# Two transformer blocks in float32 on one core: both attention stages rearranged, embedding stages reordered, and the sum of squares of retention taken earlier

## The chip, the cores and the metric

The kernel runs on one core of one Trainium2 chip. The metric is the device time of one execution in microseconds; the times given are the median of three executions and their range. The profile is of one further execution.

## The reference

Two blocks, each of two layers, work on 512 tokens of width 1024, all in float32. What matters here:

```python
# first block, layer 0: retention, 4 heads, q/k 256 wide, v 512 wide
o = o * rsqrt(mean(o * o) + eps) * gn_g          # per head, over its 512 columns
y = (silu(gate) * o) @ w_out
# first block, layer 1: latent attention, 16 heads, keys and values from one latent of width 256
q_cat = concat([q_nope @ w_uk, rope(q_rope)]) * scale
k_cat = concat([c_kv, rope(k_rope)])             # the rope part (64 wide) is shared by all heads
p = softmax(causal(q_cat @ k_cat.T)); o = (p @ c_kv) @ w_uv
# after each layer i of the first block: the embedding stage
x = x + rms_norm(y, post_norm_g[i])
x = x + (p[i] @ ple_w_proj[i]) * sigmoid(x @ ple_w_gate[i])
# second block: chunk gating mixer, MLP, then dilated attention, MLP
# dilated attention: 8 heads of 64, three groups (window, dilation) = (128,1), (512,4), (2048,16)
num = p @ v                                      # unnormalised, summed over the three groups
o = (sum of num * scale) / (sum of den * scale); y = o @ w_out
```

## The kernel before, in words

**Splitting.** Every matmul operand is split into a high part of type fp32r and a low rest, also fp32r. A product is three matmuls, high by high, high by low, low by high (`mm3`, lines 401 to 404). `tile_of` (lines 406 to 420) makes one output tile of 128 x 512 by all products with the high weights first and those with the low weights last; `tiles_together` (lines 422 to 434) makes several tiles in step, so that each part `k` of the moving operand is used by all of them before the next part is waited for.

**Panels.** All weights come as 175 panels of 128 x 2048, in the order in which they are used. SyncE loads panel `m` once the low part of `m - 2` is made; ScalarE makes the high part (`split_panel`, `split_quarter`, lines 1011 to 1026, which wait until TensorE is through with panel `m - 2`), GpSimd the low part in four quarters (line 354). Two slots for each of RAW, WH and WL.

**Engines.** There is no scheduler: each engine has its own list, written out by hand, and they meet in counting semaphores. TensorE writes 8 PSUM banks; before it takes a bank it waits until the last user has freed it (`bank`, line 379, `free`). ScalarE evicts or makes high parts (`hi`, line 1009), VectorE makes low parts (`lo`, line 1571), scales, adds and finds maxima.

**Retention** (`head`, lines 485, 1110, 1658), four times: q, k, v tiles, decayed products, gates, results. The four result tiles are squared by ScalarE, the squares added into SS by VectorE (`ret_squares`). TensorE then has gate tile 2, the matmul of ONES with SS (line 542), gate tile 3, and the two output panels, the first with `tiles_together` on YH and YL (in memory AH and AL). VectorE's order behind the sum is gate 2, reciprocal, the results times the root, low part of y(0), gate 3, and so on (lines 1717 to 1740); ScalarE's is root, tanh of gate 2, high parts of y(0) and y(1).

**Embedding** (`per_layer_input`, lines 561, 1181, 1782), after each layer of the first block: TensorE makes 8 projected tiles from panel `n` (with the sum of squares behind the second), then the gate tiles from panels `n + 1` to `n + 4`. The two tiles of `n + 1` are made together, each part k as soon as VectorE has GL(k) (24 x 512-wide matmuls per tile, 48 for both); the panels behind it come after that. ScalarE splits panel `n + 1` after the root of the norm, and the quarters of panel `n + 2` between its high parts of x.

**Latent attention** (lines 609 to 716, 1267 to 1361, 1840 to 1981), eight pairs of heads, seven of them in a loop. For a head, `mla_scores` (line 638) makes for each of four query tiles, 128, 256, 384 and 512 keys wide, three products of the latent part and three of the rope part. QRH and QRL hold the rope parts of both heads of the pair, 64 partitions each; KRH and KRL hold the key's, once for each head with the other head's partitions zeroed by OF_HEAD. At the end of a pair: `swapped` (line 619, a float32 matmul that exchanges the halves for the rotation), `latent_values`, `mla_weighted` into bank 3, and the output panel with four tiles together and four alone. VectorE's order there: low probabilities, low y(0), `turned` (line 1840: it frees the bank of the straight copy at its second multiplication), low rope, `gated`, low y(1), low values. In front of the first pair VectorE clears all of ACC (line 1882) between `turned` and low rope.

**Dilated attention** (lines 826 to 1000, 1452 to 1552, 2106 to 2289), four pairs of heads. The 36 projected tiles (`unit`) take turns in banks 0 and 1 with the transposed values (units 9 to 11 of `_unit_banks`), the exchanged sums (12) and the rows of inverses (13), each in the bank that comes next. A pair's exponentials and weighted values are made behind the units of the next pair; those of the last pair stand at the end, between the first output tiles. `att_weighted` (line 902) multiplies the values of both heads, 128 columns, with the probabilities of one, 36 matmuls per head: 9 of 256 columns moving and 27 of 128; only the 64 result partitions of the head are used.

Of the kernel before, what the change touches and what calls it, by code (L numbers as in the profile page):

```python
# [8 lines left out]
KD = D_MODEL // 128  # L9
# [79 lines left out]
def _unit_banks():  # L89


    order = []
    for n in range(ATT_PAIRS):
        if n > 0:
            order += [(n, 0), (n - 1, 11), (n, 1)]
        order += [(n, j) for j in range(2, 6)]
        if n > 0:
            order.append((n - 1, 12))
        order += [(n, 6), (n, 7)]
        if n > 0:  # L100
# [5 lines left out]
    banks[ATT_PAIRS - 1, 12], banks[ATT_PAIRS - 1, 13] = 3, 5  # L106
# [34 lines left out]
def program(nc, panels, gains, xin, pin, pos, gn, decay, consts, moves, rel, onehot, wsT, bs, out, scratch, xsave):  # L141
# [5 lines left out]
    with ctx:  # L147
# [40 lines left out]
        with ExitStack() as c:  # L188
            CQH, CQL = sb("CQH", [128, KQ, 512], f32r, c), sb("CQL", [128, KQ, 512], f32r, c)
            CKH, CKL = sb("CKH", [128, KC, 512], f32r, c), sb("CKL", [128, KC, 512], f32r, c)  # L190
            KRH, KRL = sb("KRH", [128, 2, 512], f32r, c), sb("KRL", [128, 2, 512], f32r, c)
            MQH, MQL = sb("MQH", [128, 4, 512], f32r, c), sb("MQL", [128, 4, 512], f32r, c)
            QRH, QRL = sb("QRH", [128, 512], f32r, c), sb("QRL", [128, 512], f32r, c)
# [4 lines left out]
        MU = (SS[:, :], R[:, :])  # L198
        X = sb("X", [128, KD, 512])
# [176 lines left out]
        def _(pe):  # L376
# [29 lines left out]
            def tile_of(o, w, f, width, xh, xl, k0, k1, first=True, last=True, at=0, wait=None):  # L406
# [5 lines left out]
                for k in range(k0, k1):  # L412
# [3 lines left out]
                    nc.tensor.matmul(o, wh[:, columns[k - k0]], xl[:, k, :], start=False, stop=False)  # L416
                for k in range(k0, k1):
# [50 lines left out]
            def bias_rows():  # L468
                pe.wait_ge(S["rel_loaded"], 32)
                pe.wait_ge(S["rel_neg"], 1)  # L470
# [14 lines left out]
            def head(h, first=False):  # L485
# [75 lines left out]
            def per_layer_input(L, n):  # L561
# [13 lines left out]
                for j in range(4):  # L575
                    w = panel(n + 1 + j, (n + 1 + j) % 2)
                    if j == 0:
                        ends = tiles_together([bank(0), bank(1)], w, 256, GH, GL, KD,
                                              lambda k: pe.wait_ge(S["ple_h_split"], KD * L + k + 1))
                        for f, end in enumerate(ends):  # L580
                            signal(end, "ple_gate_made", f == 1)
                        continue
# [424 lines left out]
        def _(act):  # L1007
# [10 lines left out]
            def split_quarter(m, part):  # L1018
# [6 lines left out]
                if part == 3:  # L1025
                    end.then_inc(hi_ready, 1)
# [1448 lines left out]
```

## Time and profile before

| | us |
|---|---|
| median of three executions (range) | 2277.23 (2276.5 to 2277.91) |
| the profiled execution | 2274.16 |
| its span | 2272.1 |
| TensorE matmul busy | 2177.4 (96%) |
| VectorE busy | 1187.4 (52%) |
| GpSimd busy | 969.0 (43%) |
| ScalarE busy | 861.1 (38%) |
| mean granted clock of TensorE | 0.989 |

The profiled execution took 2.1 us more than its span and 3.1 us less than the median. A busy matmul row includes the time that its result takes to arrive, so matmuls overlap: how fast they follow is read from their starts. In rows of the timeline the columns are start, duration, engine, line, operation, output and inputs, form, count, and in brackets the idle time before it with what ended it. PE is TensorE's matmuls, PEld its weight loads, DVE VectorE, ACT ScalarE, POOL GpSimd.

### The profile page before, as it was taken

The numbers are of one execution on the slowest core, as the hardware profiler recorded it, in microseconds if no ns is written. First come the engines' busy times: TensorE is split into PE (matmuls) and PEld (weight loads), VectorE is DVE, ScalarE is ACT, GpSimd is POOL, SyncE is SP. The second block draws the span as 40 slices with busy tenths as digits, with TensorE's granted clock in tenths as the row PEclk, the third lists the DMA queues.
The fourth block names the chain that finished last, engine by engine and source line by source line (L and its number), as shares of the span: only waits on it lengthen the run. The fifth ranks groups of instructions, "written<-read, shape, count | busy, mean of one in ns | idle before, by whom it ended". The sixth has DMA issues, their size and how long they took to land.

```text
span 2272.1 us, 29536 instructions
## 1 busy us (share of the span) xinstructions
PE 2177.4 (96%) x10336; PEld 1803.3 (79%) x10336; DVE 1187.4 (52%) x1714; ACT 861.1 (38%) x1264; POOL 969.0 (43%) x706
## 2 busy tenths in 40 slices
PE   7999999898999999988999999999999989999997
PEld 6888878687888888866888888887788777888885
DVE  7655556866666666667265222225465456222224
ACT  4423323544444444444444223224334444223323
POOL 4453444455433333324445544554433223544453
PEclk9999999999999999999999999999999999999998
DMA  5222222132222222212322232224221211222221
GB/s 173 86 98 79 92 78 92 66 132 92 77 82 81 74 74 74 86 72 92 113 73 95 93 105 98 92 92 130 75 75 56 75 56 56 93 92 98 105 92 56
DMA packets 37838, 200.03 MB, mean 88 GB/s; under 512 B 4331, under 2 KB 9707, under 8 KB 15372
## 3 DMA queue, kind: packets, MB, share of 16 engines
q1 hardware_dynamic: 28496, 188.76, 23.7%
q10 hardware_dynamic: 9276, 10.37, 1.5%
q8 instruction: 44, 0.72, 0.1%
q14 instruction: 22, 0.18, 0.0%
HBM read 193.87 MB, written 5.24 MB: 88 GB/s over the span
## 4 chain that ended last, share of the span: by engine, by line
PE 86%; DVE 8%; ACT 2%; DVEq 2%; issue 1%; DMA 0%; SPq 0%; ACTq 0%
PE bank L415 16%; PE bank L416 16%; PE bank L419 16%; PE bank L402 12%; PE bank L403 11%; PE bank L404 11%; ACT WH L1009 1%; PE bank L858 1%; DVE PKL L1571 1%; DVE X L1792 1%; DVE T L1790 1%; PE bank L449 1%; DVE SS L1590 1%; DVE R L1579 1%; DVE T L1719 1%
## 5 line engine op out<-in xcount | busy, mean ns | idle before, releaser
L354 POOL TENSOR_TENSOR WL<-RAW,WH 128x512 fp32r<-128x512 f32 x700 | 965.3, 1410 | 1274.4 <-ACT WH L1009 1274.4
L1009 ACT ACTIVATE WH<-RAW 128x2048 fp32r<-128x2048 f32 (+1 forms) x181 | 335.9, 1856 | 640.7 <-PE bank L419 310.2
L415 PE MATMUL bank<-HH,WH 128*128 128x512 f32 x968 | 387.6, 400 | 8.7 <-DVEq L2231 5.5
L416 PE MATMUL bank<-HL,WH 128*128 128x512 f32 x968 | 379.8, 392 | 0.0
L419 PE MATMUL bank<-HH,WL 128*128 128x512 f32 x968 | 239.1, 389 | 0.0
L415 PEld LDWEIGHTS bank<-HH,WH 128*128 128x128 f32 x968 | 183.4, 189 | 51.2 <-DVEq L2231 5.9
L416 PEld LDWEIGHTS bank<-HL,WH 128*128 128x128 f32 x968 | 183.4, 189 | 39.3 <-issue 2.2
L419 PEld LDWEIGHTS bank<-HH,WL 128*128 128x128 f32 x968 | 181.7, 188 | 37.8
L2078 DVE TENSOR_TENSOR X<-X,bank 128x512 f32<-128x512 f32 x128 | 87.7, 688 | 196.6 <-PE bank L419 117.4
L2069 DVE SCALAR_TENSOR_TENSOR TG<-bank,RS 128x512 f32<-128x512 f32 x64 | 44.0, 688 | 205.1 <-PE bank L404 135.8
L402 PE MATMUL bank<-HH,WH 128*128 128x512 f32 x288 | 112.7, 391 | 5.9 <-DVE HL L1585 5.9
L404 PE MATMUL bank<-HH,WL 128*128 128x512 f32 x288 | 112.1, 389 | 0.0
L403 PE MATMUL bank<-HL,WH 128*128 128x512 f32 x288 | 112.1, 389 | 0.0
L402 PE MATMUL bank<-HIDH,WH 128*128 128x512 f32 x256 | 99.6, 389 | 0.0
L403 PE MATMUL bank<-HIDL,WH 128*128 128x512 f32 x256 | 99.6, 389 | 0.0
L404 PE MATMUL bank<-HIDH,WL 128*128 128x512 f32 x256 | 99.6, 389 | 0.0
L415 PE MATMUL bank<-HIDH,WH 128*128 128x512 f32 x256 | 99.6, 389 | 0.0
L416 PE MATMUL bank<-HIDL,WH 128*128 128x512 f32 x256 | 99.6, 389 | 0.0
L1571 DVE TENSOR_TENSOR HIDL<-T,HIDH 128x512 fp32r<-128x512 f32 x64 | 54.7, 857 | 68.8 <-ACT HIDH L1009 65.6
L402 PE MATMUL bank<-WH,HH 128*128 128x512 f32 x192 | 74.9, 390 | 0.9 <-ACT O L1009 0.9
L404 PE MATMUL bank<-WH,HL 128*128 128x512 f32 x192 | 74.7, 389 | 0.0
L403 PE MATMUL bank<-WL,HH 128*128 128x512 f32 x192 | 74.7, 389 | 0.0
(416 smaller groups left out, 4444.6 us busy)
## 6 DMA issues: line engine op xcount, KB each, us to landing
RAW<-panels SPq DMA_DIRECT2D x175, 1024.0 KB, 4.8
X<-xin SPq DMA_DIRECT2D x4, 512.0 KB, 9.6
xsave<-X ACTq DMA_DIRECT2D x4, 512.0 KB, 2.8
X<-xsave ACTq DMA_DIRECT2D x1, 2048.0 KB, 8.5
TAB<-scratch ACTq DMA_DIRECT2D x16, 128.0 KB, 3.0
out<-ACC SPq DMA_DIRECT2D x8, 256.0 KB, 2.5
RS<-decay ACTq DMA_DIRECT2D x4, 256.0 KB, 2.5
scratch<-O SPq DMA_DIRECT2D x4, 256.0 KB
```

The source lines that it names most:

```text
L354: gp.tensor_tensor(WL[:, s, cs], RAW[:, s, cs], WH[:, s, cs].bitcast(f32), ALU.subtract).then_inc(lo_ready, 1)
L402: nc.tensor.matmul(o, ah, bh, start=start, stop=False)
L403: nc.tensor.matmul(o, ah, bl, start=False, stop=False)
L404: return nc.tensor.matmul(o, al, bh, start=False, stop=stop)
L415: nc.tensor.matmul(o, wh[:, columns[k - k0]], xh[:, k, :], start=first and k == k0, stop=False)
L416: nc.tensor.matmul(o, wh[:, columns[k - k0]], xl[:, k, :], start=False, stop=False)
L419: end = nc.tensor.matmul(o, wl[:, columns[k - k0]], xh[:, k, :], start=False, stop=last and k == k1 - 1)
L449: end = nc.tensor.matmul(o[:, :], wl[:, columns[k][i]], xh[:, k, :], start=False, stop=k == nk - 1)
L1009: return nc.scalar.activation(dst, src, ACT.Copy)
L1571: return v.tensor_tensor(dst, src, high.bitcast(f32), ALU.subtract)
L2069: v.scalar_tensor_tensor(TG[:, f % 2, :], B[f][:, :], 0.0, RS[:, :], ALU.max, ALU.mult)\
L2078: end = v.tensor_tensor(X[:, f, :], X[:, f, :], B[b][:, :], ALU.add)
```

## The change

Six things are done at once.

- Retention: the matmul of the sum of squares is issued inside gate tile 2, between its products with high and with low weights. VectorE takes gate 2 after y(0)'s low part instead of ahead of the reciprocal; ScalarE takes the tanh of gate 2 after the high parts of y(0) and y(1).
- Embedding: between the parts k of the first two gate tiles TensorE issues high products of a third tile, from the panel behind, and all of the fourth tile's high products ahead of the low ones. ScalarE loads the table of the root ahead of the squares, splits panel `n + 1` in quarters around the last square, and the quarters of `n + 2` one high part earlier each, the last one after all high parts of x.
- Latent attention, scores: QR holds for head `a` the high query part in its own 64 partitions and the low part in the other 64; KRH is not masked any more (both halves hold the same key). One matmul of QR with KRH is then high by high and low by high, and QR with the masked KRL is high by low: two matmuls for three. High and low rope parts take two instructions of 64 partitions each.
- Latent attention, order: ScalarE's straight copy frees its bank itself; five output tiles together instead of four; low rope after low y(1) on VectorE; on ScalarE high y(1) ahead of high rope and the next panel's split last; ACC cleared in two pieces, ahead of the root of the latent norm and between two low parts.
- Dilated attention, banks: values of groups 1 and 2 in banks 6 and 7, inverse rows in bank 4, so that banks 0 and 1 are left to the units, the values of group 0 and the exchanged sums. At the end, the transposes of the last pair's probabilities come right behind its last unit, and its values of group 2 after the weighted values of group 0.
- Dilated attention, weighted values: only the head's 64 value columns are loaded as weights, with the result always in partitions 0 to 63.

Two semaphores of the bias rows at the very start are merged into one.

```diff
@@ _unit_banks
-        if n > 0:
-            order += [(n, 0), (n - 1, 11), (n, 1)]
-        order += [(n, j) for j in range(2, 6)]
+        order += [(n, j) for j in range(6)]
         if n > 0:
             order.append((n - 1, 12))
-        order += [(n, 6), (n, 7)]
-        if n > 0:
-            order.append((n - 1, 13))
-        order += [(n, 9), (n, 8), (n, 10)]
-    order.append((ATT_PAIRS - 1, 11))
+        order += [(n, 6), (n, 7), (n, 9), (n, 8)]
...
+    for n in range(ATT_PAIRS):
+        banks[n, 10], banks[n, 11], banks[n, 13] = 6, 7, 4
@@ TensorE, retention
-                end = tile_of(bank(2)[:, :], w, 0, 256, HH, HL, 0, KD)
+                end = tile_of(bank(2)[:, :], w, 0, 256, HH, HL, 0, KD, between=sum_of_results)
                 end.then_inc(S["ret_g_made"], 1)
-                o = bank(4)
-                pe.wait_ge(S["ret_squares"], h + 1)
-                nc.tensor.matmul(o[:, :], ONES[:, :], SS[:, :], start=True, stop=True).then_inc(S["ret_sum"], 1)
@@ TensorE, embedding
+                for k in range(KD):
+                    pe.wait_ge(S["ple_h_split"], KD * L + k + 1)
+                    for f in range(2):
...
+                        end = mm3(os_[f][:, :], w0[0][:, c:c + 128], w0[1][:, c:c + 128], GH[:, k, :], GL[:, k, :],
+                                  k == 0, k == KD - 1)
...
+                    if k >= 2:
+                        if k % 2 == 0:
+                            pe.wait_ge(S["ple_gate_quarter"], 3 * L + k // 2)
+                        high_products(0, k - 2)
+                pe.wait_ge(hi_ready, n + 3)
+                high_products(0, KD - 2)
+                high_products(0, KD - 1)
+                os_.append(bank(3))
+                for k in range(KD):
+                    high_products(1, k)
@@ TensorE, latent attention
-                    mm3(o, QRH[:, qs], QRL[:, qs], KRH[:, a, 0:m], KRL[:, a, 0:m], False, True)\
-                        .then_inc(S["mla_s_made"], 1)
+                    nc.tensor.matmul(o, QR[:, a, qs], KRH[:, 0:m], start=False, stop=False)
+                    nc.tensor.matmul(o, QR[:, a, qs], KRL[:, a, 0:m], start=False, stop=True).then_inc(S["mla_s_made"], 1)
-                ends = tiles_together([bank(4 + f) for f in range(4)], w, 1024, MYH, MYL, 2,
+                ends = tiles_together([bank(b) for b in (4, 5, 6, 7, 1)], w, 1024, MYH, MYL, 2,
@@ TensorE, dilated attention
-                        vs = slice(128 * r, 128 * r + 128)
+                        vs = slice(128 * r + 64 * e, 128 * r + 64 * e + 64)
-                            end = mm3(o[:, rs], vh, vl, DPH[:, e, rs], DPL[:, e, rs], g == 1 and r == 0, g == 2 and r == 3)
+                            end = mm3(o[0:64, rs], vh, vl, DPH[:, e, rs], DPL[:, e, rs], g == 1 and r == 0, g == 2 and r == 3)
@@ TensorE, its end
                 unit(n, 8)
+                if n == ATT_PAIRS - 1:
+                    att_transposes(n, 0)
                 value_transposes(n, 1)
-            value_transposes(last, 2)
             os_ = [bank(0)]
             out_tile(os_[0], 0, 0, last)
-            att_transposes(last, 0)
             os_.append(bank(1))
             out_tile(os_[1], 1, 0, last)
             att_weighted(last, 0)
+            value_transposes(last, 2)
@@ ScalarE, embedding
+                nc.scalar.activation(EPSC[:, 3:4], EPSC[:, 0:1], ACT.Sqrt)
+                squares(f"post{L}", KD, y_made, lambda: split_quarter(n + 1, 0))
+                for part in range(1, 4):
+                    split_quarter(n + 1, part)
+                root(f"post{L}", D_MODEL)
...
+                for k in range(3, KD):
+                    if k % 2 == 1:
+                        split_quarter(n + 2, (k - 3) // 2, "ple_gate_quarter")
+                    high_x(k)
+                split_quarter(n + 2, 3)
@@ ScalarE, latent attention
+            def straight(b, dst):
+                nc.scalar.activation(dst, B[b][:, :], ACT.Copy).then_inc(S["mla_straight"], 1)
+                act.drain().then_inc(free[b], 1)
...
                 high_y(0)
+                high_y(1)
                 if not last:
                     act.wait_ge(S["mla_rope_f32"], n * 1 + 3)
-                    hi(QRH[:, :], TG[:, 0, :]).then_inc(S["mla_rope_hi"], 1)
-                    split_in(n, 4, N_MLA + 6)
-                high_y(1)
-                if not last:
+                    high_rope()
                     act.wait_ge(S["mla_o_made"], n * 2 + 2)
                     high_values(n + 1, (2, 0), n * 4 + (N_MLA + 5))
+                    split_in(n, 4, N_MLA + 6)
@@ ScalarE, end of dilated attention
-            high_values(last, 2)
+            high_probabilities(last, 0)
             exponentials(last, 1)
-            high_probabilities(last, 0)
             exponentials(last, 2)
             near_results(last)
+            high_values(last, 2)
@@ VectorE, latent attention
+            v.memset(ACC[:, 0:KQ, :], 0.0)
             inverse_root("ckv")
...
+            v.memset(ACC[:, KQ:KQ + KC, :], 0.0)
             low_qk(0, "k1", 2, FIRST)
-            v.memset(ACC[:, :, :], 0.0)
             low_rope(0)
...
             def low_rope(n):
+                for a in range(2):
+                    ve.wait_ge(S["mla_rope_hi"], n * 2 + (a + 2))
+                    end = lo(QR[own[1 - a], a, :], TG[own[a], 0, :], QR[own[a], a, :])
```

## Rows read from the trace of the kernel before

**Rows 1.** The page of the profile: the span, and TensorE's busy time.
```profile
span 2272.1 us, 29536 instructions
...
PE 2177.4 (96%) x10336; PEld 1803.3 (79%) x10336; DVE 1187.4 (52%) x1714; ACT 861.1 (38%) x1264; POOL 969.0 (43%) x706
```

**Rows 2.** Waits of TensorE: line, what ended them, us in all, times, longest.
```profile
PE bank L402 <- DVE GL L1571: 14.7, 12, 3.5
...
PE bank L402 <- DVE AL L1571: 5.9, 4, 1.5
...
PE bank L402 <- DVE TG L1844: 5.7, 8, 2.1
PE bank L415 <- DVEq L2231: 5.5, 3, 2.0
PE bank L402 <- DVEq L2125: 5.1, 1, 5.1
PE bank L402 <- DVE QRL L1571: 3.4, 1, 3.4
PE bank L415 <- DVEq L2112: 3.2, 7, 0.8
...
PE bank L402 <- DVE MYL L1571: 2.7, 7, 0.4
...
PE bank L837 <- DVEq L2112: 2.1, 4, 0.9
```

**Rows 3.** Timeline of retention's third head: its first output matmul.
```profile
299.98 0.49 PE L402 MATMUL bank<-AH,WH 128*128 128x512 f32 x1 [1.46 <-DVE AL L1571]
```

**Rows 4.** Timeline of the first embedding stage, VectorE.
```profile
431.10 1.53 DVE L1790 SCALAR_TENSOR_TENSOR T<-ACC,G,R 128x512 f32<-128x512 f32 x1 [0.17 <-issue]
...
438.43 0.75 DVE L1790 SCALAR_TENSOR_TENSOR T<-ACC,G,R 128x512 f32<-128x512 f32 x1
...
451.90 3.45 DVE L1571 TENSOR_TENSOR GL<-X,GH 128x512 fp32r<-128x512 f32 x2
```

**Rows 5.** Timeline of TensorE there: first gate matmul, two later tiles' first.
```profile
438.59 0.47 PE L402 MATMUL bank<-GH,WH 128*128 128x512 f32 x1 [1.80 <-DVE GL L1571]
...
456.90 0.39 PE L415 MATMUL bank<-GH,WH 128*128 128x512 f32 x1
...
462.34 0.39 PE L415 MATMUL bank<-GH,WH 128*128 128x512 f32 x1
```

**Rows 6.** Timeline of TensorE: one head's 24 score matmuls, first and next behind.
```profile
738.85 0.22 PE L402 MATMUL bank<-MQH 128*128 128x128 f32 x1
...
742.66 0.39 PE L415 MATMUL bank<-HH,WH 128*128 128x512 f32 x1
```

**Rows 7.** Timeline of VectorE at the end of a pair of latent attention.
```profile
720.71 2.38 DVE L1571 TENSOR_TENSOR PKL<-bank,PKH 128x128 fp32r<-128x128 f32 x4 [3.56 <-ACT PKH L1009]
```

**Rows 8.** Timeline of VectorE ahead of the first pair of latent attention.
```profile
564.76 3.47 DVE L1882 MEMSET ACC<- 128x4096 f32 x1 [0.80 <-issue]
```

**Rows 9.** Windows: PE, PEld, DVE, ACT, POOL busy (x), clock, DMA share, GB/s.
```profile
570.00:575.00 5.00, 5.00 (x19) 4.71 (x19) 4.07 (x10) 1.20 (x4) 5.00 (x5) 0.50 0.54 172
```

**Rows 10.** Groups by form: weight loads of 128 columns and of 24.
```profile
L403 PEld LDWEIGHTS bank<-DPL,DVH 128*128 128x128 f32 x96 | 18.4, 191 | 0.3
...
L472 PEld LDWEIGHTS bank<-TG,ST 33*24 33x24 f32 x4 | 0.3, 99 | 0.8 <-issue 0.7
```

**Rows 11.** TensorE, dilated attention: 24 of `att_weighted`, later scores with 64 rows.
```profile
1751.75 0.22 PE L402 MATMUL bank<-DPH,DVH 128*128 128x128 f32 x1
...
1754.38 0.36 PE L874 MATMUL bank<-SMR,CONST 128*128 128x32 f32 x2
...
1761.05 0.33 PE L858 MATMUL bank<-DKH,DQH 64*128 64x128 f32 x2
1761.21 0.28 PE L858 MATMUL bank<-DKL,DQH 64*128 64x128 f32 x2
```

**Rows 12.** Timeline of VectorE at the end of dilated attention.
```profile
1886.89 0.69 DVE L1571 TENSOR_TENSOR DYL<-TG,DYH 128x512 fp32r<-128x512 f32 x1 [0.70 <-ACT DYH L1009]
```

More of the change, by code:

```diff
@@ L198, in program @@
         MU = (SS[:, :], R[:, :])
+        own = [slice(64 * a, 64 * a + 64) for a in range(2)]
         X = sb("X", [128, KD, 512])
@@ L404, in mm3, with tile_of @@
                 return nc.tensor.matmul(o, al, bh, start=False, stop=stop)
-            def tile_of(o, w, f, width, xh, xl, k0, k1, first=True, last=True, at=0, wait=None):
+            def tile_of(o, w, f, width, xh, xl, k0, k1, first=True, last=True, at=0, wait=None, between=None):
                 wh, wl = w[:2]
@@ L416, in tile_of @@
                     nc.tensor.matmul(o, wh[:, columns[k - k0]], xl[:, k, :], start=False, stop=False)
+                if between is not None:
+                    between()
                 for k in range(k0, k1):
@@ L574, in per_layer_input @@
                         end.then_inc(S["sines"], 1)
-                for j in range(4):
-                    w = panel(n + 1 + j, (n + 1 + j) % 2)
[L577 to L582, printed above, removed]
+                w0, w1 = panel(n + 1, (n + 1) % 2), panel(n + 2, (n + 2) % 2)
@@ new lines, in per_layer_input @@
+                pe.wait_ge(hi_ready, n + 3)
[4 more added lines that the diff above has]
+                    high_products(1, k)
+                for f in range(2):
+                    for k in range(KD):
+                        c = 256 * k + 128 * f
+                        low_up_to(w1, c)
+                        end = nc.tensor.matmul(os_[2 + f][:, :], w1[1][:, c:c + 128], GH[:, k, :], start=False, stop=k == KD - 1)
+                    signal(end, "ple_gate_made", f == 1)
@@ L583, in per_layer_input @@
+                for j in range(2, 4):
+                    w = panel(n + 1 + j, (n + 1 + j) % 2)
                     for f in range(2):
@@ L705, in pair @@
                 w = panel(out_, s1)
-                ends = tiles_together([bank(4 + f) for f in range(4)], w, 1024, MYH, MYL, 2,
+                ends = tiles_together([bank(b) for b in (4, 5, 6, 7, 1)], w, 1024, MYH, MYL, 2,
                                       lambda k: pe.wait_ge(S["mla_y_split"], n * 2 + (k + 1)))
                 for f in range(KD):
-                    end = ends[f] if f < 4 else tile_of(bank((1, 3, 0, 2)[f - 4])[:, :], w, f, 1024, MYH, MYL, 0, 2)
+                    end = ends[f] if f < 5 else tile_of(bank((3, 0, 2)[f - 5])[:, :], w, f, 1024, MYH, MYL, 0, 2)
                     signal(end, "mla_out_made", f == KD - 1)
@@ L1026, in split_quarter @@
                     end.then_inc(hi_ready, 1)
+                elif sig is not None:
+                    end.then_inc(S[sig], 1)
             def split_at(m):
@@ L1033, in split_in, with squares @@
                 split_panel(i * per + m0, m0 % 2, i * (per // 2) + m0 // 2)
-            def squares(name, n, ready):
+            def squares(name, n, ready, in_front_of_last):
                 for k in range(n):
+                    if k == n - 1:
+                        in_front_of_last()
                     src = ready(k)
@@ L1282, in _ @@
             act.wait_ge(panel_used, N_MLA)
-            straight(B[0][:, :], T[:, 2, :])
+            straight(0, T[:, 2, :])
             root("ckv", KV_LORA)
@@ L1854, in low_rope @@
             def low_rope(n):
-                ve.wait_ge(S["mla_rope_hi"], n * 1 + 3)
-                lo(QRL[:, :], TG[:, 0, :], QRH[:, :]).then_inc(S["mla_rope_split"], 1)
+                for a in range(2):
+                    ve.wait_ge(S["mla_rope_hi"], n * 2 + (a + 2))
+                    end = lo(QR[own[1 - a], a, :], TG[own[a], 0, :], QR[own[a], a, :])
+                end.then_inc(S["mla_rope_split"], 1)
             def low_values(n, banks):
@@ L2223, in numerators @@
                     far, near = in_order(B[6 + e], 1), natural(NEAR[:, e, :], 1)
-                    v.tensor_tensor(natural(NUM, 1)[own], near[own], far[own], ALU.add).then_inc(free[6 + e], 1)
+                    v.tensor_tensor(natural(NUM, 1)[own], near[0:64], far[0:64], ALU.add).then_inc(free[6 + e], 1)
                 ve.drain()
```

97 lines of the change are left out of this document (51 added, 46 removed).

## The prediction

> **What bounds the kernel.** I read the page first. TensorE's matmuls are busy for 2177 us of a span of 2272 [rows 1], so what counts is how many matmuls there are, how fast they follow each other, and where TensorE waits. It takes its instructions in order. The second view is the list of waits with TensorE as the one that waits [rows 2]: few are long, and those that this change touches are the twelve for GL in the embedding stages, four for AL in retention, those for TG, MYL and QRL in latent attention, and those that VectorE's queue ends at lines 2231, 2125 and 2112 in dilated attention. The third view is the timeline, for starts. Two tiles of 24 matmuls with 512 columns begin 5.44 us apart [rows 5], so one such matmul costs 5.44 / 24 = 0.227 us. I use start to start throughout, since the duration in a row (0.39) overlaps the next. ScalarE, VectorE and GpSimd are busy half the time or less; they matter only where their chain ends a wait.
>
> The sum is made against the profiled execution, 2274.2 us: its span and 2.1 us around it. The median of the runs is 3.1 us above that, and the saving is taken from the median.
>
> **Retention, 6.0 us.** The output panel waits 1.46 us for y(0)'s low part [rows 3], 5.9 us over four heads [rows 2]. The matmul of the sum now comes ahead of the tile's 8 products with low weights, 8 x 0.227 = 1.8 us earlier; behind it VectorE has one operation of about 0.7 us less before y(0), ScalarE a tanh less. 1.8 + 0.7 is more than 1.46, so the wait goes, with a slower first matmul behind it: 1.5 a head. What is late next is y's parts 2 and 3, each one VectorE operation of some 0.7 us behind the last while TensorE has three matmuls a part and tile; and the squares, needed 1.8 us earlier now. Bounds: 1.0 to 1.6 a head, 4 to 6.5.
>
> **Embedding stages, 12.0 us.** The first two gate tiles begin at 438.59 and their 48 matmuls end at 456.90 [rows 5]: 18.3 us, where 48 x 0.227 = 10.9 would do. The 7.4 us are steps at VectorE's pace, one GL after the other, with 1.8 ahead of the first. The change puts 2 high products of a third tile (0.45 us) behind each part from the third on and 8 more behind, work that TensorE would do anyhow: all 16 fill 16 x 0.227 = 3.6 us of gaps. The rest comes from the quarters of panel `n + 1` going earlier, so that GpSimd's splits lie ahead of VectorE's first operations: with GpSimd busy T takes 1.53 us, without 0.75, and two GL take 3.45 [rows 4]. Three or four such operations give 2 to 3 us, and the high products leave the low ones of the first two tiles to start later, when the last GL is there. Against it: the table of the root is loaded ahead of the squares (which I put at about 1, a guess between nothing and the 1.8 that TensorE waits there), and ScalarE gets a quarter between two squares. 5.6 and 6.4 for the two stages. Bounds: 3.6 a stage, only the products, 7; both stages without a gap, 16.
> Beside the row there is a rule. The Trainium skill, "SBUF — State Buffer", on the engine side, says that VectorE with two SBUF inputs and GpSimd lock their shared port pair for a whole instruction and the loser blocks; 1.53 against 0.75 agrees in kind. By it a split moved away is won in full, which is the upper bound.
>
> **Latent attention, 20.3 us.** A head's scores are 24 matmuls in 742.66 - 738.85 = 3.81 us [rows 6]. One in six goes: 3.81 / 6 = 0.635, for two heads 1.27 a pair. The waits in seven pairs: TG, because the straight copy frees its bank only after VectorE's multiplication, which stands behind low probabilities (2.38 us, themselves 3.56 late [rows 7]), and MYL [rows 2]; (5.7 less the longest, 2.1, which stands before the first pair) / 7 = 0.52, and 2.7 / 7 = 0.39. Freed by ScalarE, and with a fifth output tile of 6 matmuls (1.4 us) between the parts of y, both go; so do two slow restarts, 0.1 each. 1.27 + 0.52 + 0.39 + 0.2 = 2.4, times 7 is 16.7. What moves: low rope goes behind low y(1) on VectorE and waits for ScalarE's high rope, behind which nothing of this pair's output stands; it is due at the next pair's scores, some 7 us on by the timeline. The next panel's high part is last on ScalarE, and GpSimd's quarters behind it, due at the next pair's first `tile_of` [rows 6]. Two instructions of 64 partitions for one of 128 cost up to 0.7 more on VectorE and on ScalarE, under the same cover; without it 1.4 a pair. Last pair: the scores of its first head, 0.6; those of the second lie behind VectorE's maxima.
> Before the first pair TensorE waits 3.4 for QRL and 2.1 for TG [rows 2]. ACC's clearing, 3.47 us right ahead of low rope [rows 8], is moved where VectorE waits. TG's wait and QRL's hang on one chain, so they don't add: about 3.5 less 0.7 for the second rope instruction is 3. The clock is granted at 0.50 there [rows 9], behind the waits, and I leave that as it is. Bounds 1.3 and 4.3. 16.7 + 0.6 + 3 = 20.3.
>
> **Dilated attention, bank order: 10.5 us.** L415 waits 5.5 us for VectorE at 2231 and 3.2 at 2112, line 837 2.1 at 2112 [rows 2]: units and transposes whose bank is still being read. With values and inverses in banks 6, 7 and 4 the units' turn is free of them. 10.8 less 0.6 for what recurs, and 0.3 for restarts. Bounds 5 and 12.
>
> **Dilated attention, narrow weights: 7.0 us.** A head has 9 matmuls of 256 moving columns and 27 of 128, 8 heads, 216 of the latter. 24 of them take 2.63 us, 0.110 each [rows 11], about as long as one with 256 moving columns, so it is the weight load that sets their pace. Loads take 191 ns for 128 columns and 99 for 24 [rows 10], 0.88 ns a column: 56 ns less for 64. 0.110 - 0.056 is 0.054, and 216 x 0.056 = 12. The 72 with 256 columns keep 0.12. A quarter lies in the last pair, whose end is costed below. No row shows 64-column weights. Switches of shape do have rows: scores with 64 rows follow each other by 0.16 after a switch, against 0.11 [rows 11]; 24 stretches of weighted values, two switches each, 0.05 each, is 2.4, of which I take 2 off: (12 x 3 / 4) - 2 = 7. Bounds: 0, no quicker, and 11.
> The Trainium skill speaks against this part twice in "TensorEngine Tiling (Array Packing)": by Key Properties a changed tiling mode drains TensorE, and by Restrictions column tiling disables Fast Weight Load. The first is what the 0.05 shows; by the second a 64-column load might be no quicker than the present 128, which no row here shows, and which is the first rival.
>
> **Dilated attention, its end: 7.0 us.** DYL of the last pair ends at 1887.6 [rows 12], and TensorE had stood 5.1 for the bank at 2125 [rows 2]. The transposes of the last probabilities come behind the last unit instead of behind the first output tile, and the values of group 2 behind the weighted values of group 0. The 5.1 go, and narrow weights shorten what the last chain holds by 4 stretches, some 3 to 4 us. Against it exponentials and low probabilities are needed earlier and TensorE waits there: of 9 I take 7. Bounds 3 and 9. The merged semaphore at the start: nothing, it is a wait on DMA in both.
>
> **Sum.** 6.0 + 12.0 + 20.3 + 10.5 + 7.0 + 7.0 = 62.8; profiled 2211.4, median 2277.2 - 62.8 = 2214.4. I take 2215. All parts good: 6.5 + 16 + 22 + 12 + 11 + 9 = 76.5, 2201. Parts of the sum poor together: 4 + 8 + 16 + 5 + 4 + 3 = 40, 2237.
>
> **Rivals.**
> (1) *Narrow weights load no quicker*. For: no row has them, and the durations of loads overlap matmuls, so 0.88 ns a column is soft. Against: the 0.110 a matmul, with only 128 columns to move, is as slow as with 256, so something else than the moving side sets it, and the load is what is left. Then 7.0 and about 2 in the end go: 2215 + 9 = 2224. Chance 0.15.
> (2) *A wait for the next late item takes the removed one's place*: in the embedding stages the high products wait for a quarter that GpSimd hasn't made, so the change doesn't do what it says there; in a pair TensorE stands for ScalarE's high y(1) or the next panel; in the units for the evicted tile. For: in all these VectorE and ScalarE run at TensorE's pace. Against: they are busy 52 and 38% [rows 1]. Half of embedding (6), the waits of the pairs (7 x 0.9 = 6), 5 of banks, 5 of the end: 22 less, 2237. Chance 0.13.
> (3) *Slower than before*: with 64-column weights a load no longer runs beside the matmul ahead. Place: the 288 matmuls of `att_weighted`; price: 0.19 load [rows 10] + about 0.27 matmul - 0.11 = 0.35 each, 101 us, so 2215 + 9 + 101 = 2325. It makes the sum positive from (62.8 - 9) / 288 = 0.19 us a matmul. Against: scores with 64 rows do overlap [rows 11]. Chance 0.03.
>
> **Chances.** Forecast 0.68, (1) 0.15, (2) 0.13, (3) 0.03; 0.01 for a mishap that leaves the time as it was. A measurement of this kernel can tell some 0.2%, 4.6 us. Forecast, (1) and (2) are all faster: 0.96, same 0.01, slower 0.03. Range: 2200, with all parts good, to 2239, which holds (1) and most of (2).
>
> **Signs in the profile after.** AL gone from TensorE's waits. From first gate matmul to the end of the stretch with the 16 high products about 15 to 16 us (10.9 + 3.6 + 1). A head's scores in 3.17 us, 20 matmuls. TG, MYL, lines 2231 and 2112 gone or under 1. QRL under 1. 24 weighted matmuls in 1.4 us; weight loads of 64 columns at 135 ns. DYL of the last pair 9 us nearer to the stage's start. It would be wrong if PE waits under 402 name GpSimd's quarters, if the stretch of 24 still takes 2.6 us, or if a matmul with narrow weights shows its load in the open.

## The result, and the profile after

The changed kernel took 2204.68 us (median of four runs, 2201.23 to 2208.47), the one before 2276.86; the ratio is 0.9683, with a 95% interval of 0.9665 to 0.9702. Five further runs of it had a median of 2206.72. The forecast was 2215, the range 2200 to 2239. The profiled execution took 2208.5, its span is 2206.7; that of before was 2272.1, so the two profiles differ by 65.4 us, the medians by 72.2.

The page of the changed kernel, head and TensorE's busy time [rows 1]:

```profile
span 2206.7 us, 29453 instructions
...
PE 2148.6 (97%) x10272; PEld 1781.6 (81%) x10272; DVE 1183.2 (54%) x1724; ACT 869.0 (39%) x1279; POOL 960.6 (44%) x706
```

TensorE's waits in the changed kernel (line, what ended them, us in all, times, longest), the head of the list and what answers to [rows 2]:

```profile
PE bank L445 <- ACT WH L1046: 10.4, 1, 10.4
PE bank L401 <- DVE HL L1630: 5.9, 5, 1.7
PE bank L401 <- DVE QR L1616: 5.9, 1, 5.9
...
PE bank L932 <- ACT LG L1522: 2.5, 2, 1.6
...
PE bank L401 <- issue: 1.5, 2, 1.4
...
PE bank L401 <- DVE GL L1616: 1.0, 2, 0.6
...
PE bank L414 <- DVEq L2161: 0.8, 1, 0.8
```

GL fell from 14.7 to 1.0. AL, TG, MYL and the two entries of DVEq with 5.5 and 5.1 are gone; of the 5.3 us at line 2112 0.8 is left. One wait grew: QR before the first pair of latent attention, 5.9 where QRL had 3.4; the prediction's signs had it under 1. It is the place where the waits for T and TG were gathered up (1.9, 2.1 and 3.4 before, one of 5.9 now). Two waits are new, both at the end of dilated attention: 2.5 for LG, ScalarE's exponentials, and one of 1.4 at 1811.7, in front of the weighted values of group 1, which take VectorE's low probabilities.

To see where the time went, I matched the runs of TensorE's matmuls of the two timelines by their operands and compared the starts. Each stage begins and ends at such a start:

| stretch | before, us | after, us | difference | forecast |
|---|---|---|---|---|
| to retention's first scores | 61.74 | 63.42 | +1.7 | 0 |
| retention, to the first embedding stage | 361.34 | 354.91 | -6.4 | -6.0 |
| embedding stage 0, to the norm sum of the next stage | 77.34 | 71.39 | -6.0 | -5.6 |
| from there to the first gate tile of latent attention | 75.20 | 72.48 | -2.7 | -3.0 |
| latent attention from there, to the second embedding stage | 433.67 | 414.29 | -19.4 | -17.3 |
| embedding stage 1 | 77.74 | 70.59 | -7.1 | -6.4 |
| mixer and first MLP | 483.19 | 483.33 | +0.1 | 0 |
| dilated attention, to the last sums' transposes | 272.15 | 255.43 | -16.7 | -17.5 |
| its end, to the MLP | 85.40 | 75.57 | -9.8 | -7.0 |

What is left, +0.9, lies in the last 25 us. The rows are all near their terms. Whether the terms are right inside is what the experiments were for, and there several did not hold. One shift belongs to the borders: the stretch to the first gate tile of latent attention ends behind the scores of the first head, whose saving (0.7 of the 2.7) the forecast books under the pairs.

The +1.7 at the start is not the change's. A window at 40 to 45 us has the granted clock at 0.66, and the same kernel, profiled again, has it at 1.00 (columns as in [rows 9]; first fence the first profile, second fence the second):

```profile
40.00:45.00 5.00, 5.00 (x15) 4.03 (x16) 4.70 (x5) 2.77 (x2) 3.36 (x3) 0.66 0.60 211
```
```profile
40.00:45.00 5.00, 5.00 (x23) 4.10 (x23) 4.58 (x6) 2.65 (x3) 3.56 (x3) 1.00 0.52 202
```

Fifteen matmuls in the five microseconds against 23, TensorE busy for all five in both. Just ahead, both profiles have the same wait of 0.88 us for ScalarE's O, ended at 39.9 and 39.7. Everything behind that stretch lies at the same distance in both profiles to 0.15 us.

### The profile page after: what moved, and what is told of

Same layout as the page of the kernel before. It is cut to its first block, busy times and chain, and to the rows that moved or that the text cites. A ratio compares the mean times of both kernels' runs of the same rounds, so it can differ in the third digit from the quotient of the medians.

```text
span 2206.7 us, 29453 instructions
## 1 busy us (share of the span) xinstructions
PE 2148.6 (97%) x10272; PEld 1781.6 (81%) x10272; DVE 1183.2 (54%) x1724; ACT 869.0 (39%) x1279; POOL 960.6 (44%) x706
## 4 chain that ended last, share of the span: by engine, by line
PE 87%; DVE 7%; DVEq 2%; ACT 2%; issue 1%; DMA 0%; ACTq 0%
PE bank L414 15%; PE bank L415 15%; PE bank L420 15%; PE bank L401 12%; PE bank L403 12%; PE bank L402 12%; DVE SS L1635 1%; PE bank L893 1%; PE bank L686 1%; PE bank L445 1%; PE bank L446 1%; DVE X L1849 1%; PE bank L450 1%; DVE T L1846 1%; DVEq L1634 1%
```

## The experiments

Each kernel below is the changed one with one thing undone or altered. The profile tells more than the times here: nine runs of the changed kernel lie between 2201.2 and 2208.5, with a median of 2206.7, while a stage of its timeline repeats to 0.1 us where the clock does. The runs on scores, on the pair, on ACC's clearing in one piece and on retention were made on another chip than the rest; the kernel before took 2274.28 there (median of seven) and 2275.39 and 2276.89 on the chip of the others, so a difference of 1 or 2 us between their times and those nine is not read.

### Narrow weights

```diff
-vs = slice(128 * r + 64 * e, 128 * r + 64 * e + 64)
-... mm3(o[0:64, rs], vh, vl, ...)
+vs = slice(128 * r, 128 * r + 128)
+... mm3(o[:, rs], vh, vl, ...)
```

> The changed kernel with 128 value columns loaded as weights again in att_weighted, all else as changed. My theory: a weight load sets the pace of matmuls with 128 moving columns, so 24 of them take 2.63 us instead of 1.44, the pairs get 2.7 us longer each and the whole about 10.8 longer: 2215.5. Rival, narrow weights cost switches elsewhere that this gets back: under 8 longer.

Measured: 2217.06 (2214.07 to 2221.15), 10.3 above the nine runs, as expected. Each of the first three pairs is longer by 0.33 + 1.19 + 1.19 = 2.71 us, at the three places where `att_weighted` stands: 8.1 for 18 stretches. The last pair adds 5.0, of which 2.7 is the same; the rest goes with a stretch at half clock (0.50 at 1820 to 1825) which the changed kernel does not have there.

In the changed kernel, timeline of TensorE, the 24 matmuls of [rows 11], first and next behind, and below them groups by form, of the changed kernel:

```profile
1703.75 0.22 PE L401 MATMUL bank<-DPH,DVH 128*64 128x128 f32 x1
...
1705.19 0.36 PE L909 MATMUL bank<-SMR,CONST 128*128 128x32 f32 x2
```
```profile
L402 PE MATMUL bank<-DPL,DVH 128*64 128x128 f32 x72 | 13.7, 223 | 0.0
...
L402 PEld LDWEIGHTS bank<-DPL,DVH 128*64 128x64 f32 x96 | 12.9, 135 | 0.6
```

1.44 us for 24, 0.060 each, against 0.110. A load of 64 columns is recorded at 135 ns, as the line through 191 and 99 gave [rows 10]. Is it still the load that sets the pace?

```diff
-vs = slice(128 * r + 64 * e, 128 * r + 64 * e + 64)
+vs = slice(128 * r + 64 * e, 128 * r + 64 * e + 32)
```

> The changed kernel with 32 of a head's 64 value columns loaded as weights; the other 32 are left out of the result. If at 64 columns the load still sets the pace, 24 matmuls with 128 moving columns fall from 1.44 us to about 0.8; if the moving side does now, they stay at 1.4, and the whole stays within 1 us.

Half of each head's values is left out of the result. Groups by form of this kernel:

```profile
L402 PE MATMUL bank<-DPL,DVH 128*32 128x128 f32 x72 | 13.8, 224 | 0.0
...
L402 PEld LDWEIGHTS bank<-DPL,DVH 128*32 128x32 f32 x96 | 10.4, 108 | 1.0
```

The loads are shorter by 27 ns and nothing else moves: the 24 matmuls start at 1703.85, the next one at 1705.29, 1.44 us again, and the span is 2206.6. The time, 2208.41 in two runs, is 1.7 above the nine and that of the first profile of the changed kernel, 2208.47; both have the stretch at low clock at 40 us. At 64 columns the load no longer sets the pace; that the moving side does is what is left, not shown by itself. With 128 moving columns the pace stays at 0.060, and 0.050 a matmul was to be had, not 0.056.

### Banks of dilated attention

```diff
 order += units 0 to 5, exchanged sums, units 6, 7, values 0, unit 8
+order += values of groups 1 and 2, inverse rows    (each in its old place, pairs 0 to 2)
-banks[n, 10], banks[n, 11], banks[n, 13] = 6, 7, 4
```

> The changed kernel with the old turn of banks 0 and 1 for values of groups 1 and 2 and the inverse rows in pairs 0 to 2 (the end keeps its banks). My theory: the waits for the bank at units and value transposes come back, about 8 us in three pairs: 2213. Rival, most of that gain was something else, such as a stretch at half clock that no longer comes: 3 us or less.

Measured: 2220.88 (2217.76 to 2222.43), 14.2 more, well above the expectation of 8. Its waits of TensorE:

```profile
PE bank L420 <- DVEq L2286: 8.9, 3, 3.1
...
PE bank L420 <- DVEq L2167: 3.2, 7, 0.8
...
PE bank L878 <- DVEq L2167: 1.2, 3, 0.4
```

These are lines 2231 and 2112 of before [rows 2], and the first is not the 5.5 us it was. A unit tile waits there for the bank of the inverse rows, which VectorE frees at its own time, some 24 weighted matmuls later. When these became 1.19 shorter, TensorE came 1.19 earlier and waited so much longer: 5.5 / 3 = 1.8, 8.9 / 3 = 3.0. At these three places, six of the 24 stretches, narrow weights alone would have brought next to nothing. Bank order and narrow weights are each worth more with the other.

The three entries of the list are 13.3 us, where the changed kernel has 0.8; the wait of 2.5 for LG is gone in return. In the profile the time from dilated attention's first value transposes (1581.4 here, 1588.1 in the changed kernel) to the MLP behind it is 290.2 us against 273.4, 16.9 longer. Some 5 us of that is clock, by my estimate from the granted clock over these stretches (0.86 at 1648 to 1660, where the changed kernel has 1.00, and 0.87 over the 40 us at 1790 to 1830, where it has 0.96 at 1780 to 1820), which leaves about 12 for the banks. The profiled execution is the shortest of the four all the same, 2217.76, 11.0 above the nine: the stretch at low clock at 1565 to 1575, worth 3.2, is missing ahead in it. So the stage is read from the profile and not from the median.

### The order at the end

```diff
-att_transposes(last, 0); value_transposes(last, 1); out tiles 0, 1; att_weighted(last, 0); value_transposes(last, 2)
+value_transposes(last, 1); value_transposes(last, 2); out tile 0; att_transposes(last, 0); out tile 1; att_weighted(last, 0)
```

and ScalarE's and VectorE's lists to match.

> The changed kernel with the old order at the end of dilated attention on TensorE, ScalarE and VectorE (narrow weights and banks as changed). My theory: 4 to 8 us longer, since TensorE waits for probabilities again before the output tiles, 2209 to 2213. Rival, the banks alone took the 5 us wait away and the order does nothing: within 1.5 us.

Measured: 2207.38 (2206.72 to 2208.18), within 0.7 us of the nine runs. In the profile the MLP begins 0.4 us earlier than in the changed kernel. The rival is right about the time: the order does nothing that these runs can tell. The wait of 5.1 us at line 2125 [rows 2] is gone with the old order and gone with 128-column weights, so neither is its cause alone and the banks are what is left; no run gave the last pair its old banks. The wait that my theory named does come back, 2.75 us at 1805.9 for the low probabilities, but others pay for it. In the changed kernel the moved transposes stand 2.5 us for LG and the weighted values of group 1 another 1.4; with the old order:

```profile
PE bank L932 <- ACT LG L1522: 2.5, 2, 1.6
```
```profile
PE bank L401 <- issue: 2.9, 2, 2.8
...
PE bank L932 <- ACT LG L1521: 0.9, 1, 0.9
...
PE bank L872 <- DVE UFS L2159: 0.7, 1, 0.7
```

(the first of the changed kernel, the second of this one). The waits from the last sums' transposes to the last DYL are 4.9 us in the changed kernel and 5.4 here; this profile has no stretch at low clock at 1796 to 1806, where the changed kernel has 0.83. The changed end is 9.8 us shorter than before by banks, by 2.7 of narrow weights, and by clock: 1845 to 1855 and 1855 to 1870 were granted 0.83 and 0.77 before, while the changed kernel has 0.83 in the 10 us at 1796 to 1806 and 1.00 behind.

### Embedding

```diff
-squares(..., lambda: split_quarter(n + 1, 0)); quarters 1 to 3; root; ...     # all of it as before
-TensorE: high products of tiles 3 and 4 between and ahead
+tiles_together([bank(0), bank(1)], ...) and tile_of for the others
```

> The changed kernel with both embedding stages as before (no early high products of tiles 3 and 4, ScalarE's quarters and table load as before). My theory: 12 to 13 us longer, 6 and 7 a stage: 2217.5. Rival, part of it is a stretch at half clock in the second stage that comes or not by itself: 10 or less.

and with TensorE's list alone as before:

> The changed kernel with TensorE's old order in the embedding stages (two tiles in step, then the third and fourth alone), ScalarE's order as changed. My theory: the sixteen high products filled gaps, 3.6 us a stage, so 6 to 7 longer than the changed kernel and 6 shorter than with the whole stage undone. Rival: the quarters and the table alone bring it and the products only move a wait, under 3 longer; or they bring nothing and it is 12 longer.

All undone: 2221.87 (2220.47 to 2222.15), 15.2 more. Stage 0 is longer by 7.8, stage 1 by 7.1, more than the 12 to 13 expected. In stage 0 that is 1.8 more than before had: the window 445 to 455 is granted 0.83 here, and was at full clock before.

TensorE's list alone undone: 2203.61 (2203.38 to 2203.85), not longer at all. Stage by stage it is 0.7 and 1.4 longer, 2.1 in both, where 6 to 7 were expected. The median is even 3.1 below that of the nine runs: two stretches at low clock are missing here (1565 to 1575 and 1796 to 1806), and with the first alone its stage is 3.2 shorter. The rival is right here too. VectorE's timeline shows why. First the stage with everything undone, then with only TensorE's list undone:

```profile
425.19 1.54 DVE L1806 SCALAR_TENSOR_TENSOR T<-ACC,G,R 128x512 f32<-128x512 f32 x1 [0.17 <-issue]
426.80 1.63 DVE L1808 TENSOR_TENSOR X<-X,T 128x512 f32<-128x512 f32 x1
...
444.41 1.65 DVE L1808 TENSOR_TENSOR X<-X,T 128x512 f32<-128x512 f32 x1
445.99 3.43 DVE L1587 TENSOR_TENSOR GL<-X,GH 128x512 fp32r<-128x512 f32 x2
```
```profile
425.02 0.79 DVE L1806 SCALAR_TENSOR_TENSOR T<-ACC,G,R 128x512 f32<-128x512 f32 x1 [0.17 <-issue]
425.89 0.69 DVE L1808 TENSOR_TENSOR X<-X,T 128x512 f32<-128x512 f32 x1
...
441.40 1.47 DVE L1587 TENSOR_TENSOR GL<-X,GH 128x512 fp32r<-128x512 f32 x2
```

The first four operations take 6.4 us, 2.9 with ScalarE's changed order; the last three 5.1 and 2.2. That is 6.4 us off the chain that TensorE follows, in one stage. What stands beside the first four is GpSimd's low parts of panel `n + 1`, which in the second kernel end at 425.3, as the chain begins:

```profile
424.89 6.39 POOL L353 TENSOR_TENSOR WL<-RAW,WH 128x512 fp32r<-128x512 f32 x4 [10.84 <-ACT WH L1017]
```
```profile
420.27 5.00 POOL L353 TENSOR_TENSOR WL<-RAW,WH 128x512 fp32r<-128x512 f32 x4 [6.38 <-ACT WH L1017]
```

Beside the last three are those of `n + 2`, from 444.2 on; in the second kernel they begin at 442.8, when the chain is through. All seven operations that meet a quarter of GpSimd's are longer by 0.7 to 1.0 us, and the first four quarters of GpSimd's by 1.4 together. The Trainium skill, "SBUF — State Buffer", on the two separate sides, says that VectorE with two SBUF inputs and a GpSimd instruction that reads SBUF take an exclusive lock on the port pair they share, each for its whole instruction, and whichever comes second is blocked. The rows agree in kind: both lose time, GpSimd's quarter takes 1.6 instead of 1.25 us and no operation of VectorE's waits longer than that; how far into a quarter each one came they don't show.

With the chain that early only 0.55 us a part is left to fill, seen ten times in the two stages (0.4 once):

```profile
PE bank L401 <- DVE GL L1587: 5.4, 10, 0.6
```

The high products fill these: the first four gate tiles are through 1.8 us earlier in either stage. In stage 0 1.1 of it is given back a little later: with them TensorE waits 0.72 for HL, one of the five in the list of the result, and restarts slowly; without them it doesn't. In stage 1 0.4 goes the same way.

### Latent attention: scores, pair, entry

```diff
+nc.tensor.matmul(o, QR[:, a, qs], KRL[:, a, 0:m], start=False, stop=False)    # scores: this matmul twice
```

> The changed kernel with a third rope matmul a key product again: the one of QR with KRL is done twice (the output then has that low part twice). My theory: it is TensorE's time and nothing else, 0.63 us for each of 15 heads and about nothing for the second head of the last pair: 9.5 to 10 longer, 2214. Rival: the extra time fills waits that are there anyway, under 5.

Measured: 2212.55 (2210.79 to 2214.46). In the profile 9.8 longer at the transposes behind the last head's scores and 8.8 at the second embedding stage; the last head's part is hidden, as expected. The time is only 5.8 above the nine runs; 3.2 of the difference is the stretch at low clock at 1565 to 1575, which is missing here. In the changed kernel a head's 20 matmuls [rows 6] take 3.17 us:

```profile
717.77 0.22 PE L401 MATMUL bank<-MQH 128*128 128x128 f32 x1
...
720.94 0.40 PE L414 MATMUL bank<-HH,WH 128*128 128x512 f32 x1
```

```diff
-straight(3, ...) frees bank 3; tiles_together of 5; low_rope behind low_y(1)
+turned(...) frees bank 3; tiles_together of 4; low_rope ahead of gated(1, 3) and low_y(1); high_y(1) behind high_rope and the next panel's split
```

> The changed kernel with the old order inside a pair of latent attention: VectorE frees the straight copy's bank, four output tiles together, low rope ahead of gated and low y(1), high y(1) behind high rope. My theory: the waits TG and MYL come back with their restarts, 1.1 to 1.4 a pair, 8 to 10 in seven pairs: 2213.5. Rival: with two rope instructions the old order is worse than before, over 12.

Measured: 2220.51 (2216.72 to 2221.63), 13.8 more: 2.3 us a pair in the profile (55.17 against 52.91), 0.8 at TG's wait and 1.5 at MYL's, restarts included, so the rival holds. Its waits:

```profile
PE bank L401 <- DVE MYL L1616: 8.2, 7, 1.2
PE bank L401 <- DVE TG L1890: 6.2, 8, 2.6
...
PE bank L401 <- DVE QR L1616: 0.7, 1, 0.7
```

MYL waits 1.2 a pair instead of 0.4 [rows 2]. The two low rope operations, of 64 partitions each, take 1.38 us together, two thirds of a microsecond more than the one with 128, and in the old order they stand ahead of low y(1). The prediction had named that as the price without cover. The new order is what makes the saved score matmul free of it.

```diff
-v.memset(ACC[:, 0:KQ, :], 0.0) ahead of the root; v.memset(ACC[:, KQ:KQ + KC, :], 0.0) between low parts
+v.memset(ACC[:, :, :], 0.0)    # between turned and low rope
```

> The changed kernel with ACC cleared in one piece between the turned rope and low rope, as before. My theory: 2.5 to 3 us longer ahead of the first pair: 2207.5. Rival: the clearing was beside ScalarE's high rope and GpSimd's split, and what held QR was the two contended half operations: 1 or less.

Measured: 2208.30 (2207.85 to 2209.84), 1.6 more, and 0.7 longer at QR in the profile, which is all that its timeline differs in up to TensorE's last matmul: the rival. The clearing stood where VectorE waited for ScalarE's high rope anyway. What does hold QR, VectorE and GpSimd in the changed kernel:

```profile
549.57 1.46 DVE L1890 TENSOR_TENSOR TG<-TG,COS 128x512 f32<-128x512 f32 x1
551.11 1.59 DVE L1892 TENSOR_TENSOR TG<-TG 128x512 f32<-128x512 f32 x1
553.39 2.65 DVE L1616 TENSOR_TENSOR QR<-TG,QR 64x512 fp32r<-64x512 f32 x2 [0.69 <-ACT QR L1046]
```
```profile
549.19 6.30 POOL L353 TENSOR_TENSOR WL<-RAW,WH 128x512 fp32r<-128x512 f32 x4 [9.90 <-ACT WH L1046]
```

It is the same meeting as in the embedding stages, and the same remedy was tried:

```diff
-split_at(N_MLA + 2)
 act.wait_ge(S["mla_rope_f32"], 2)
 high_rope()
+split_at(N_MLA + 2)
```

with ACC's second piece cleared between the turned rope and low rope.

> The changed kernel, and ahead of the first pair of latent attention ScalarE splits the next panel behind the two high rope operations instead of ahead, and ACC's second piece is cleared between the turned rope and low rope. My theory: GpSimd's low parts of that panel stretch four of VectorE's operations in QR's chain, 1.46, 1.59 and 2.65 for two; without them QR comes 2.5 to 3 earlier and the wait of 5.9 is under 3.3; if the half clock behind it goes too, up to 5 in all. Rival: ScalarE's or VectorE's own pace holds QR, or the panel is now late for the first gate tile: within 1.

```profile
548.72 0.68 DVE L1890 TENSOR_TENSOR TG<-TG,COS 128x512 f32<-128x512 f32 x1
549.48 0.69 DVE L1892 TENSOR_TENSOR TG<-TG 128x512 f32<-128x512 f32 x1
550.34 0.91 DVE L1931 MEMSET ACC<- 128x1024 f32 x1 [0.16 <-issue]
551.26 1.38 DVE L1616 TENSOR_TENSOR QR<-TG,QR 64x512 fp32r<-64x512 f32 x2
```

QR's wait is 2.4 instead of 5.9, the first scores start 3.4 us earlier:

```profile
PE bank L401 <- DVE QR L1616: 2.4, 1, 2.4
```

Measured: 2201.19 (2199.78 to 2205.53), beside 2206.72 for the changed kernel on the same chip; the ratios to before are 0.9666 (0.9653 to 0.9679) and 0.9685 (0.9672 to 0.9698). These intervals overlap, so the times alone don't settle it; the timelines do for that place, and 2.9 us of it reach the end. The half clock behind the wait stays (0.77 over 547 to 562).

> The changed kernel as it is, for more runs beside the next ones. Its four runs so far lay between 2201.2 and 2208.5, wider than those of before. If stretches at half clock that come or not make that spread, its profile has others of them than the first one had, at 40 to 45 and 1565 to 1575 us above all, and the rest of the stretches agree within 0.1 us.

Half of it came true. The stretch at 40 to 45 was different, as shown, and nothing else was: 1565 to 1575 was at 0.66 in the first profile and low again in this one. Its five runs are 2206.7 to 2207.0 four times and 2201.5 once.

### Retention

```diff
-end = tile_of(..., between=sum_of_results)
+end = tile_of(...); sum_of_results()    # gate 2 and its tanh back ahead of y(0)
```

> The changed kernel with retention as before. My theory: 1.5 to 1.6 us a head, 6 to 6.4 longer in all: 2211, and the profile shows four waits for AL again. Rival: the wait would move to y's parts 2 and 3, so that less than 4 us is at stake.

Measured: 2212.77 (2209.31 to 2213.45), 6.1 more; in the profile 6.2 at the first embedding stage, 6.4 from retention's first scores to there. The four waits are back:

```profile
PE bank L401 <- DVE AL L1617: 5.9, 4, 1.5
```

In the changed kernel the output matmul of [rows 3] follows on its predecessor without a wait.

## Why the prediction was right, and which steps were not

- **The bound and the sum.** TensorE set the time, and matmuls and waits taken from it came off nearly one for one. 62.8 us were forecast and the profiles show 65.4; the medians show 72.2, because the changed kernel's profiled execution is the longest of its four and holds the 1.7 at the start. By the nine runs and the kernel before beside the last five (2276.89) it is 70.2. The result lies 10 below the forecast, inside the range. That the total came so near is in part luck: the terms for embedding, entry and end were near in size for reasons that did not hold, and some of the gain in the table is granted clock, which no term had (embedding stage 1 was granted 0.98 before and 1.00 now, the end 0.94 and 0.98).
- **Retention: right.** 6.0 forecast, 6.4 shown by the change and by undoing it.
- **Embedding: the size right, its parts wrong.** That all 16 high products fill 3.6 us of gaps a stage failed: they bring 1.8 and keep 0.7 and 1.4. (From the first gate matmul to the end of the 16 it is 16.3 and 17.8 us, where the signs had 15 to 16.) "Three or four such operations give 2 to 3 us" was short: seven operations met GpSimd, and they gave 6.4 of VectorE's chain. Two errors of opposite sign. The gap that the high products were to fill had been made by the very operations that another step of the change freed. The extra table load, put at 1, cost nothing that shows: R is ready at the same distance in both.
- **Pairs of latent attention: right, a little short.** 2.76 a pair against 2.4. The scores gave 1.3 as computed; the waits with their restarts 1.5, where I had 1.1: a restart costs about 0.3 and not 0.1 (TG's wait was 0.52 on the list and 0.8 came off, MYL's 0.39 and 0.7).
- **Entry: the size off by a third, the cause wrong.** 2.7 for 3, of which 0.7 is the first head's shorter scores, so 2.0 at the first scores' start. The clearing, for which it was mostly booked, is 0.7. In the kernel with the old pair order, where VectorE frees the straight copy's bank, the first scores start 1.0 later than in the changed one if the 1.7 at the start is allowed for; behind them it is ahead, by the granted clock (last section). The contention that remained was worth 3.4 more.
- **Banks: the waits right, the size short.** The term was 10.5 by the list of waits. With narrow weights present it is about 12, since they lengthen three of the waits that it removes (5.5 to 8.9), and low clock that goes with the waits comes on top: 14.2 by the medians, 16.9 in the profile.
- **Narrow weights: the mechanism right, the size nearly.** 8.1 for three pairs against 7.0. No load came into the open, and the switches didn't cost the 2 taken off. Rival 1 and rival 3 are out: the rows show 135 ns against 191 for a load, and 0.060 against 0.110 from matmul to matmul. The Trainium skill, "TensorEngine Tiling (Array Packing)", Restrictions, says that column tiling disables Fast Weight Load. Whether that was on for the wide weights no run shows; the narrow load is the quicker one here.
- **End: wrong in its cause.** The term was the wait of 5.1, which I gave to transposes and order, and 3 to 4 of narrow weights, less what comes against them. The order is worth nothing within what these runs can tell; 9.8 went by the banks, by 2.7 of narrow weights and by less time at half clock.
- **Rival 2** was right in small places (HL behind embedding stage 0, LG and the low probabilities in the end) and not in size.

Open: the exact shares of the entry, for freeing by ScalarE was undone only together with the pair's order; and why three experiments (the ones on scores, on banks, and on TensorE's embedding list alone) have no low clock at 1565 to 1575, which is worth 3.2 us there, though the wait of 2.0 us for DKL ahead of it is the same in all. With neither that nor the one at 1796 the last of these has its four runs at 2203.4 to 2203.9, below seven of the changed kernel's nine. Whether the high products have a part in that I can't say; so the times don't show that they are worth having.

## What to carry to other kernels

Before filling a gap of the bounding engine, ask whether the gap is there once the other steps of the change are made: look at the durations of the operations that the engine waits for, and whether they double where GpSimd works beside them. An edit that makes a stretch shorter just ahead of a wait is worth nothing until the wait is gone (at three places here waits of 5.5 us in all became 8.9), so waits behind a stretch are removed with it and counted together. And of a change with many parts a good sum proves none of them; undo them one at a time and read the stage, not the total.

## What the runs showed of the hardware that was not expected

- One wait of 5.9 us is followed by half clock, the lower of the two levels, in part of the next ten microseconds (0.54 and 0.78 at 555 to 565); in the kernel with the old pair order the idle time lies in three waits of 1.9, 2.6 and 0.7, the clock is at 0.67 in 550 to 555, and 555 to 565 is at full clock. From the first scores to the first gate tile that kernel takes 3.3 us, the changed one 6.0, so TensorE gained 2.7 us back. First fence the changed kernel, second the one with the old order:

```profile
555.00:560.00 5.00, 3.83 (x15) 3.83 (x16) 4.00 (x7) 3.49 (x4) 1.99 (x3) 0.54 0.57 211
560.00:565.00 5.00, 5.00 (x19) 4.01 (x19) 4.01 (x13) 2.67 (x8) 3.52 (x3) 0.78 0.16 23
```
```profile
555.00:560.00 5.00, 4.53 (x26) 4.11 (x27) 3.85 (x9) 4.05 (x5) 2.67 (x2) 1.00 0.49 151
560.00:565.00 5.00, 5.00 (x24) 4.14 (x23) 4.23 (x12) 2.29 (x6) 3.84 (x4) 1.00 0.16 64
```

- The clock also falls behind a wait of only 0.88 us, TensorE busy for 4.1 of the five microseconds up to 40 and for all of the five that follow: 15 matmuls instead of 23 from 40 on, in one profile of the changed kernel and not in the other, which has the same wait. It is worth 1.7 to 1.8 us.
- Weighted matmuls with 128 moving columns follow each other by 0.110 us with 128 columns of weights, and by 0.060 with 64 and with 32. With 256 moving columns it is 0.120 with 128 columns of weights and 0.116 with 64.
